# The decode stage of a hybrid attention step: order of loads, masks on another engine, softmax in pieces

## Chip, core and metric

The kernel runs on one core of a Trainium2 chip. The metric is the device time of one execution in microseconds (us). Names of engines: PE is TensorE (PEld its weight loads), DVE is VectorE, ACT is ScalarE, POOL is GpSimd, SP is SyncE, which issues plain DMAs. All data of the stage in question is 32-bit floating point.

## What is computed

One step of a decoder layer: attention in three branches (compressed, selected, local window), a state-space branch, and an MLP, for a prompt of 1024 tokens and for 8 sample sequences of 4 new tokens each behind 4096 cached ones. The change lies in the samples' attention, cut here to what matters:

```
kc = compress(k_all, ...); vc = compress(v_all, ...)                  # 255 compressed rows a sequence
o_cmp, p_cmp = attend_shared(q, kc, vc, dist, dist >= 0, table)
idx, ok = select_blocks(jnp.sum(p_cmp, axis=2), q_pos, ...)           # 16 of the 64-row blocks
o_slc = slc_sample(q, k_slc, v_slc, idx, ok, q_pos, cache_k_slc, cache_v_slc, layer, page_table, table)
o_win, nbk, nbv = win_sample(q, k_win, v_win, cache_k_win[layer], cache_v_win[layer], q_pos, past_len, table)

def masked_softmax(s, mask):
    s = jnp.where(mask, s, NEG_INF)
    p = jnp.where(mask, jnp.exp(s - jnp.max(s, axis=-1, keepdims=True)), 0.0)
    return p / jnp.maximum(jnp.sum(p, axis=-1, keepdims=True), TINY)
```

The kernel computes the selected branch densely: scores against all 4096 cached keys, a mask that is added for the blocks not chosen, one softmax over 4128 columns (32 of them for the new rows), and products with all cached values.

## The kernel before

The stages run one after the other, each ending at a barrier of all engines: inputs, state-space, projections, compression, prompt attention, decode (`stage_decode`), tail (mixing, MLP, output). Only decode and a small preparation of gather indices in `table_steps` are touched.

Decode treats the 8 sequences as two halves of 4 (`NBAT`, `M`; in the text half 0 and half 1, `b` in the code). The rows of a half's score tiles `Ss[b]` (selected, 128 x 4128), `Sw[b]` (window, 128 x 544) and `Sc[b]` (compressed, 128 x 256) are its 4 sequences times 32 queries.

Keys. SP loads the local window of each sequence (256 KB) into four slots `kwin`, the profile's vslc and kT, in runs of one 512-byte row. POOL gathers the paged keys and values with indirect DMAs of 1 MB, 128 rows of 8 KB (16 tokens each), into a ring of 8 slots (`ring`, the last one in the profile under the name bt). There are 32 such gathers: 0 to 7 are half 0's keys, 8 to 15 half 1's, 16 to 23 half 0's values, 24 to 31 half 1's. Gathers 0 to 7 wait for nothing; 8 to 23 wait until PE has turned the keys in their slot, 24 to 31 until the value products have read it (`values_read`). SP's queue holds the windows in order: half 0's keys, half 1's keys (each when its slot is turned), half 0's values, half 1's values.

Key loop. For each half there are nine groups `y`: group 0 is the window, groups 1 to 8 take a quarter of a ring slot of each of the four sequences. PE transposes 16 blocks of 128 x 128 into four PSUM banks (L1913, `keys`), ACT copies three of the banks to SBUF (L2036, the profile calls the target qT) and DVE one (L2086, `keep_keys`). PE then multiplies queries with the turned keys of the group before (L1923, `scores`), and DVE copies the 128 x 512 scores out (L2092, `evac`). Groups 1 to 4 read gathers 0 to 3 (8 to 11 for half 1), groups 5 to 8 the next four.

Between the copies stand, in each engine's own written order: first scores with compressed and new keys (`first_scores`), the sums that rank the blocks (`block_sums`, DVE, on `Sc`), the window's bias, maximum and weights, the choice of blocks (`select`). When half 0's last scores are kept, DVE adds the bias of the last columns (`tail_bias`, L2128) and the masks (`selected`, L2133, twice 2048 columns). Half 0's maximum over 4128 columns (`top`, L2070), its exponential on ACT (`softmax`, L2022) and its scaling (`weights`, L2067) stand in half 1's key loop, at groups 4, 5 and 7.

Values. PE transposes the 40 blocks of a half's weights (`turn`, L1945), ACT and DVE copy them out by turns (`keep_turned`, L2027 and L2015), and PE multiplies them with compressed, window and gathered values (L1978). Half 1's own mask, maximum, exponential and scaling run while PE does half 0's products:

```
            act.wait_ge(scores_done, 2 * GRP)
            keep_turned(0)
            softmax(1, 2, Ss[1][:, :])
            act.wait_ge(values_done, 1)
            keep_turned(1)
```

## Time and profile before

| | us |
|---|---|
| median of 3 runs | 2231.59 (2225.74 to 2232.64) |
| span of the profiled execution | 2226.2 |
| decode in it, first DMA to the tail's first | 918.27 to 1052.73 |
| PE busy over the span | 2067.7 (93%) |
| DVE, ACT, POOL busy over the span | 906.0, 767.3, 559.4 |

The page gives the profiled execution by its span, from the first to the last instruction; no other time of it is noted. The span lies 5.4 us below the median of the runs.

How to read it: PE's 93% is an average that the long products of the tail and the projections set. Decode is some 134 us, in which no engine is busy throughout, and it is read from the timeline (start, duration, engine, line, operation, and in brackets how long the engine stood before it and whom it waited for) and from tables of stretches.

### The profile page before, as it was taken

To read this page: it belongs to the slowest core of one execution; us is meant where nothing else is said; L and a number is where in the kernel's file an instruction comes from. 1 tells how busy PE (TensorE), PEld (TensorE's weight loads), DVE (VectorE), ACT (ScalarE), POOL (GpSimd) and SP (SyncE) were. 2 spreads that over 40 slices of the span, in tenths; PEclk is the share of its full clock that TensorE was granted. 3 is DMA by queue.
4 is the path that set the end of the run, shared out by engine and by line. 5 is a ranking of instruction groups with operands and counts; after the bars stand their busy time and mean duration, and the time that the engine had idled before them with its cause. 6 is when DMAs were issued, how large, how long until landed. Compare 5 with 4: busy or idle time off the path is not lost.

```text
span 2226.2 us, 33758 instructions
## 1 busy us (share of the span) xinstructions
PE 2067.7 (93%) x13984; PEld 1864.4 (84%) x13984; DVE 906.0 (41%) x1720; ACT 767.3 (34%) x1557; POOL 559.4 (25%) x455
## 2 busy tenths in 40 slices
PE   6978899889979999686999999999999999999997
PEld 4755599878856767455999999999999999999997
DVE  4764131146566677375411124454124214313414
ACT  4130321145546777452422232333013113202313
POOL 0640000055433554322212212112212221222120
PEclk8976889989978999799999999999999999999999
DMA  9203035275313223566411113111111111111111
GB/s 354 90 1 121 10 71 114 48 265 193 148 45 84 77 57 83 206 248 258 134 48 48 43 44 116 43 44 38 49 47 48 48 40 46 48 48 38 48 58 78
DMA packets 217072, 201.97 MB, mean 91 GB/s; under 512 B 37174, under 2 KB 199966, under 8 KB 208264
## 3 DMA queue, kind: packets, MB, share of 16 engines
q1 hardware_dynamic: 205126, 131.82, 20.4%
q0 software_dynamic: 9216, 67.11, 7.9%
q8 instruction: 111, 1.82, 0.3%
q10 hardware_dynamic: 2578, 0.88, 0.2%
q14 instruction: 41, 0.34, 0.1%
HBM read 178.05 MB, written 21.58 MB: 90 GB/s over the span
## 4 chain that ended last, share of the span: by engine, by line
PE 51%; DMA 1%; DVE 0%; ACT 0%; POOL 0%; SPq 0%; issue 0%; ACTq 0%; DVEq 0%
PE ps L2216 17%; PE ps L2214 17%; PE ps L2215 17%; PE ps L2360 1%; DMA tail<-x_keep 1%; PE ps L2381 0%; DMA tail<-in_w_br_ssm 0%; POOL tail L2612 0%; DVE tail L2701 0%; SPq L2326 0%; ACT tail L2545 0%; DVE tail L2643 0%; ACT tail L2459 0%; ACTq L2241 0%; ACT tail L2489 0%
## 5 line engine op out<-in xcount | busy, mean ns | idle before, releaser
L2214 PE MATMUL ps<-tail,tail 128*128 128x356 f32 (+2 forms) x2304 | 756.6, 328 | 9.7 <-POOL tail L2612 9.7
L2216 PE MATMUL ps<-tail,tail 128*128 128x356 f32 (+2 forms) x2304 | 750.5, 326 | 0.0
L2215 PE MATMUL ps<-tail,tail 128*128 128x356 f32 (+2 forms) x2304 | 748.6, 325 | 0.0
L2612 POOL TENSOR_TENSOR tail<-tail,tail 128x1024 fp32r<-128x1024 f32 x96 | 232.3, 2420 | 924.6 <-ACT tail L2459 924.6
L2214 PEld LDWEIGHTS ps<-tail,tail 128*128 128x128 f32 x2304 | 435.4, 189 | 12.4 <-POOL tail L2612 9.9
L2215 PEld LDWEIGHTS ps<-tail,tail 128*128 128x128 f32 x2304 | 435.6, 189 | 2.5
L2216 PEld LDWEIGHTS ps<-tail,tail 128*128 128x128 f32 x2304 | 435.8, 189 | 0.0
L2459 ACT ACTIVATE tail<-tail 128x1024 fp32r<-128x1024 f32 x96 | 101.0, 1053 | 320.6 <-PE ps L2216 314.6
L2643 DVE SCALAR_TENSOR_TENSOR tail<-ps,mod,tail 128x346 f32<-128x346 f32 (+2 forms) x120 | 68.7, 573 | 346.7 <-PE ps L2216 336.6
L1669 POOL TENSOR_SCALAR pr<-pr,row_reciprocals,gT 128x640 f32<-128x640 f32 (+7 forms) x128 | 98.7, 781 | 144.7 <-DVE row_reciprocals L1795 142.1
L2514 ACT ACTIVATE tail<-tail,tail 128x346 f32<-128x346 f32 (+2 forms) x96 | 55.9, 583 | 195.5 <-DVE tail L2683 100.1
L1364 DVE TENSOR_TENSOR x_lo<-ps,x_hi 128x512 fp32r<-128x512 f32 (+1 forms) x136 | 85.9, 671 | 80.6 <-ACT x_hi L1328 79.7
L2626 DVE TENSOR_TENSOR tail<-tail,tail 128x346 f32<-128x346 f32 (+2 forms) x48 | 28.9, 601 | 208.9 <-ACT tail L2479 208.9
L2677 DVE TENSOR_TENSOR tail<-ps,tail 128x346 f32<-128x346 f32 (+2 forms) x96 | 50.4, 525 | 154.1 <-PE ps L2216 95.1
L1328 ACT ACTIVATE x_hi<-ps 128x512 fp32r<-128x512 f32 (+1 forms) x136 | 72.7, 582 | 89.2 <-PE ps L1283 89.0
L1730 ACT ACTIVATE pr<-ps,nmax 128x640 f32<-128x640 f32 (+7 forms) x128 | 90.1, 704 | 22.0 <-DVE nmax L1774 20.6
L2214 PE MATMUL ps<-h_lo,w_hi 128*128 128x352 f32 x264 | 88.9, 337 | 9.3 <-DVE w_lo L1154 9.3
L1774 DVE TENSOR_REDUCE nmax<-ps 128x1 f32<-128x640 f32 (+7 forms) x128 | 90.6, 708 | 4.5
L1593 PE MATMUL ps<-consts,pr 128*128 128x128 f32 (+6 forms) x592 | 90.1, 278 | 0.2
L2216 PE MATMUL ps<-h_hi,w_hi 128*128 128x352 f32 x264 | 87.9, 333 | 0.0
L2215 PE MATMUL ps<-h_hi,w_lo 128*128 128x352 f32 x264 | 87.9, 333 | 0.0
L1283 PE MATMUL ps<-consts,byg 128*128 128x128 f32 (+1 forms) x544 | 72.3, 278 | 12.8 <-DMA byg<-out 7.2
(489 smaller groups left out, 2988.7 us busy)
## 6 DMA issues: line engine op xcount, KB each, us to landing
tail<-in_w_ff SPq DMA_DIRECT2D x64, 512.0 KB, 3.9
wada_late<-in_w_ada SPq DMA_DIRECT2D x32, 512.0 KB, 4.0
wada<-in_w_ada SPq DMA_DIRECT2D x4, 2048.0 KB, 11.9
tail<-in_w_in SPq DMA_DIRECT2D x16, 512.0 KB, 3.6
x_keep<-xT SPq DMA_DIRECT2D x1, 4224.0 KB, 23.8
h_keep<-hT SPq DMA_DIRECT2D x1, 4224.0 KB, 11.5
tail<-x_keep SPq DMA_DIRECT2D x1, 4224.0 KB, 13.7
xrow<-in_x_prompt SPq DMA_DIRECT2D x8, 512.0 KB, 8.4
```

The source lines that it names most:

```text
L1283: mm = pe.transpose(bank[y % 4][:, o:o + m], byg[0:m, i % 2, half, g, s:s + 2, :].rearrange("p s d -> p (s d)"), e.ident[0:m, 0:m])
L1328: act.activation(to, src, ACT.Copy).then_inc(hi_kept, 1)
L1364: dve.tensor_tensor(to, src, move(i, b, xhi)[1], ALU.subtract).then_inc(lo_kept, 1)
L1593: mm = pe.transpose(b[0:n, (t % 4) * P:(t % 4 + 1) * P], pr[:, u % NPR, t * n:(t + 1) * n], e.ident)
L1669: pool.tensor_scalar(p, p, rinv[:, k:k + 1], gT[:, qb, h:h + 1], ALU.mult, ALU.mult).then_inc(scaled, 1)
L1730: act.activation(p, score(s), ACT.Exp, bias=nmax[:, s % 4:s % 4 + 1], accum_out=rsum[:, sum_at(s):sum_at(s) + 1]).then_inc(exps_done, 1)
L1774: dve.tensor_reduce(nmax[:, u % 4:u % 4 + 1], s, AXX, ALU.max, negate=True).then_inc(maxima_done, 1)
L2214: pe.matmul(out, whi[:, kw, :], xlo(kx), start=(i == 0), stop=False)
L2215: pe.matmul(out, wlo[:, kw, :], xhi(kx), start=False, stop=False)
L2216: mm = pe.matmul(out, whi[:, kw, :], xhi(kx), start=False, stop=(i == n - 1))
L2459: act.activation(whi[:, x % 2], wraw[:, x % 2], ACT.Copy).then_inc(w_hi, 1)
L2612: pool.tensor_tensor(wlo[:, x % 2], wraw[:, x % 2], whi[:, x % 2], ALU.subtract).then_inc(w_split, 1)
```

## The change

Six things, all in decode but the first:

- `table_steps` makes a second table of row indices, `rowfine`, for half-size rows of 4 KB (8 tokens): index 2r for the first half of row r, 2r+1 for the second, for the columns of gathers 0 to 3.
- The windows of keys and values are laid out with four successive tokens in a partition, so that SP's loads move runs of 2 KB. The window's bias and mask are added with the columns in that order.
- POOL waits for the four first windows before it issues a gather. Gathers 0 to 3 are each split in two, the four first halves ahead of the four second ones. PE waits for the first halves at group 1 and for the second ones at group 3.
- The masks and the tail's bias move from DVE to POOL, into its queue of gathers: behind gathers 11, 15, 19 and 23.
- Maximum and exponential of the 4128 columns are cut in four (`partial_max`, `join_max`, `part`). Half 0's pieces stand between the key copies of half 1's groups 3 to 5 (maxima) and 6 to 8 (exponentials); the scaling follows the loop (`join_sums`, two pieces). Half 1's maxima and exponentials stand ahead of `keep_turned(0)`.
- PE turns a half's weights before it waits for the outputs of the half before.

The diff, cut to its core:

```
+        early = pf[:, 0:2 * FINE].rearrange("p (m h) -> p m h", h=2)[:, :, 0]
+        for s in range(2):
+            dve.tensor_scalar(pfine[:, s, :], early, 2.0, float(s), ALU.mult, ALU.add).then_inc(row_index_step, 1)
+        dve.wait_ge(row_index_step, 5)
+        dve.tensor_copy(e.rowfine[:, :], pfine[:, :, :].rearrange("p s m -> p (s m)")).then_inc(row_index_step, 1)
...
-                sp.dma_start(slots[n % M], cache[0, n].rearrange("(j p) g d -> p j (g d)", p=P)).then_inc(landed[n % M], 16)
+                sp.dma_start(slots[n % M], cache[0, n].rearrange("(p j) g d -> p j (g d)", j=4)).then_inc(landed[n % M], 16)
...
+            def mask(b, half):
+                v = Ss[b][:, half * PAST // 2:(half + 1) * PAST // 2].rearrange("p (s j c) -> p s j c", s=CHK, c=4)
+                k = scs[b][:, half * 32:half * 32 + 32].unsqueeze(1).unsqueeze(3).to_broadcast([P, CHK, 32, 4])
+                pool.wait_ge(selection_step[b], 2)
+                if half == 0:
+                    pool.wait_ge(scores_kept, GRP * b + 5)
+                else:
+                    pool.wait_ge(scores_kept, GRP * (b + 1))
+                    last = Ss[b][:, PAST // 2:PAST].rearrange("p (s c) -> p s c", c=P)[:, :, P - 8:P]
+                    pool.tensor_tensor(last, last, e.btail[:, :].rearrange("p (c s) -> p s c", s=CHK), ALU.add).then_inc(tails_added, 1)
+                    pool.wait_ge(tails_added, b + 1)
+                pool.tensor_tensor(v, v, k, ALU.add).then_inc(masked, 1)
+
+            for m in range(M):
+                load_wait(pool, window_keys_landed[m], 1)
+            for s in range(2):
+                for m in range(M):
+                    pool.indirect_dma_start(ring[m][:, s * CHK // 2:(s + 1) * CHK // 2, :].rearrange("p s x -> p (s x)"), None, fine_rows,
+                                            bass.IndirectOffsetOnAxis(ap=e.rowfine[:, s * M + m:s * M + m + 1], axis=0))\
+                        .then_inc((first_halves, ring_landed)[s][m], 16)
+            for x in range(M, NBAT * 16):
...
+                if 8 <= x < 24 and m == M - 1:
+                    mask((x - 8) // 8, half)
...
-                    elif (y - 1) % 4 == 0:
+                    elif b == 0 and y == 1:
+                        load_wait(pe, first_halves[m], 1)
+                    elif (y - 1) % 4 == 0 or (b == 0 and y == 3):
...
             for b in range(NBAT):
+                for y in range(NG):
+                    turn(b, y)
                 if b:
                     pe.wait_ge(outputs_kept, b)
                 pe.wait_ge(selection_step[1], 2)
-                for y in range(NG):
-                    turn(b, y)
...
+            def part(b, i):
+                act.wait_ge(maxima_done[b], 3)
+                s = Ss[b][:, i * QW:(i + 1) * QW]
+                act.activation(s, s, ACT.Exp, bias=st[:, b, 2:3], accum_out=parts_sum[:, b, i:i + 1]).then_inc(exps_done[b], 1)
...
-                    if b and y == 5:
-                        softmax(0, 2, Ss[0][:, :])
+                    if b and y >= 6:
+                        part(0, y - 6)
+            part(0, 3)
             act.wait_ge(scores_done, 2 * GRP)
+            for i in range(4):
+                part(1, i)
             keep_turned(0)
-            softmax(1, 2, Ss[1][:, :])
...
+            def partial_max(b, i):
+                dve.wait_ge(masked, 2 * b + (1 if i < 2 else 2))
+                dve.tensor_reduce(mx[:, b, i:i + 1], Ss[b][:, (0, 1024, 2048, 3072, W)[i]:(0, 1024, 2048, 3072, W)[i + 1]], AXX, ALU.max).then_inc(partial_maxima, 1)
...
+                if b:
+                    partial_max(0, 0)
                 for y in range(4, GRP):
-                    if b and y == 4:
-                        top(0, 2, Ss[0][:, :])
-                    if b and y == 7:
-                        weights(0, 2, Ss[0][:, :])
                     keep_keys(b, y)
                     evac(b, y - 1)
+                    if b and y == 4:
+                        partial_max(0, 1)
+                    if b and y == 5:
+                        partial_max(0, 2)
+                        partial_max(0, 3)
+                        join_max(0)
                 evac(b, GRP - 1)
-                if b == 0:
-                    tail_bias(0)
-                    selected(0, 0)
-                    selected(0, 1)
+            join_sums(0)
+            for i in range(4):
+                partial_max(1, i)
+            join_max(1)
             dve.wait_ge(scores_done, 2 * GRP)
             keep_turned(0)
-            tail_bias(1)
-            selected(1, 0)
-            selected(1, 1)
-            top(1, 2, Ss[1][:, :])
-            weights(1, 2, Ss[1][:, :])
+            join_sums(1)
             outputs(0)
```

How the instructions stand on the engines that the rest of the text speaks of. POOL in decode, before: the 32 gathers, keys (in_cache_k_slc) and then values (in_cache_v_slc), nothing else.

```order
L1892 DMA ring<-in_cache_k_slc,rowidx 128x2048 x7
L1892 DMA bt<-in_cache_k_slc,rowidx 128x2048
L1892 DMA ring<-in_cache_k_slc,rowidx 128x2048 x7
L1892 DMA bt<-in_cache_k_slc,rowidx 128x2048
L1892 DMA ring<-in_cache_v_slc,rowidx 128x2048 x7
L1892 DMA bt<-in_cache_v_slc,rowidx 128x2048
```

POOL in decode now, up to the first mask of half 1: eight half gathers through rowfine, then whole ones with the masks (Ss with scs) and the tail's bias (Ss with btail) between them.

```order
L1917 DMA ring<-in_cache_k_slc,rowfine 128x1024 x8
L1927 DMA ring<-in_cache_k_slc,rowidx 128x2048 x3
L1927 DMA bt<-in_cache_k_slc,rowidx 128x2048
L1927 DMA ring<-in_cache_k_slc,rowidx 128x2048 x4
L1911 TENSOR_TENSOR Ss<-Ss,scs 128x2048
L1927 DMA ring<-in_cache_k_slc,rowidx 128x2048 x3
L1927 DMA bt<-in_cache_k_slc,rowidx 128x2048
L1909 TENSOR_TENSOR Ss<-Ss,btail 128x16x8
L1911 TENSOR_TENSOR Ss<-Ss,scs 128x2048
L1927 DMA ring<-in_cache_v_slc,rowidx 128x2048 x4
L1911 TENSOR_TENSOR Ss<-Ss,scs 128x2048
```

Each mask stands behind four gathers and ahead of the next four. ACT from the middle of half 1 on, before: L2036 copies keys, L2022 is a softmax's exponential, L2027 copies turned weights.

```order
L2036 ACTIVATE qT<-ps 128x512 x9
L2022 ACTIVATE Ss,st<-Ss,st 128x4128
L2036 ACTIVATE qT<-ps 128x512 x9
L2027 ACTIVATE qT<-ps 128x512 x4
L2027 ACTIVATE wt_end<-ps 128x512
L2022 ACTIVATE Ss,st<-Ss,st 128x4128
L2027 ACTIVATE qT<-ps 128x512 x4
L2027 ACTIVATE wt_end<-ps 128x512
```

ACT now, from the first piece of half 0's exponential on: L2080 copies keys, L2066 is a piece, L2071 copies turned weights.

```order
L2066 ACTIVATE Ss,parts_sum<-Ss,st 128x1032
L2080 ACTIVATE qT<-ps 128x512 x3
L2066 ACTIVATE Ss,parts_sum<-Ss,st 128x1032
L2080 ACTIVATE qT<-ps 128x512 x3
L2066 ACTIVATE Ss,parts_sum<-Ss,st 128x1032 x6
L2071 ACTIVATE qT<-ps 128x512 x4
L2071 ACTIVATE wt_end<-ps 128x512
L2071 ACTIVATE qT<-ps 128x512 x4
L2071 ACTIVATE wt_end<-ps 128x512
```

Six pieces stand in a row: the last two of half 0 and all four of half 1, ahead of the first copies of turned weights. DVE at the end of half 1's key loop, before: the last score copies (L2092), half 0's turned weights (L2015), then half 1's tail bias, masks and maximum.

```order
L2092 COPY Ss<-ps 128x512 x2
L2015 COPY qT<-ps 128x256
L2015 COPY qT<-ps 32x128
L2015 COPY qT<-ps 128x128
L2015 COPY qT<-ps 128x512 x3
L2015 COPY wt_end<-ps 128x384
L2015 COPY wt_end<-ps 32x128
L2128 TENSOR_TENSOR Ss<-Ss,btail 128x16x8
L2133 TENSOR_TENSOR Ss<-Ss,scs 128x2048 x2
L2070 TENSOR_REDUCE st<-Ss 128x1
```

DVE there now: L2138 is the score copy, L2183 to L2189 sum and scale half 0, L2175 and L2179 are half 1's maxima and their join, L2054 copies half 0's turned weights.

```order
L2138 COPY Ss<-ps 128x512 x2
L2183 TENSOR_REDUCE st<-parts_sum 128x1
L2185 TENSOR_SCALAR st<-st 128x1
L2186 RECIPROCAL st<-st 128x1
L2189 TENSOR_SCALAR Ss<-Ss,st,gate_columns 128x2048
L2189 TENSOR_SCALAR Ss<-Ss,st,gate_columns 128x2080
L2175 TENSOR_REDUCE mx<-Ss 128x1 x4
L2179 TENSOR_REDUCE st<-mx 128x1
L2054 COPY qT<-ps 128x256
L2054 COPY qT<-ps 32x128
L2054 COPY qT<-ps 128x128
L2054 COPY qT<-ps 128x512 x3
```

Half 0's scaling has moved from inside the loop to its end, and half 1's maxima from behind half 0's turned weights to ahead of them.

## Rows read from the trace of the kernel before

**Rows 1.** Stretches: length, busy us by engine (instructions), PE clock, DMA share, GB/s.

```profile
917.50:941.00 23.50, 4.78 (x28) 3.26 (x29) 2.05 (x7) 1.19 (x2) 7.59 (x8) 0.60 0.92 359
...
930.00:932.00 2.00, 1.11 (x4) 0.71 (x4) 0.00 (x0) 0.35 (x1) 0.00 (x0) 0.50 1.04 429
```

**Rows 2.** Timeline, key windows: start, length, engine, line, operation [stood before, for].

```profile
918.27 1.71 SPq L1870 DMA_DIRECT2D vslc<-in_cache_k_win  x3
...
921.74 0.66 PE L1913 MATMUL ps<-consts,vslc 128*128 128x128 f32 x4 [2.21 <-DMA vslc<-in_cache_k_win]
...
940.30 1.11 PE L1913 MATMUL ps<-consts,kT 128*128 128x128 f32 x4 [8.69 <-DMA kT<-in_cache_k_win]
```

**Rows 3.** Timeline of POOL's gather issues, and L1892's summary of issue to landing.

```profile
918.96 1.04 POOL L1892 DMA_INDIRECT ring<-in_cache_k_slc,rowidx  x1 [6.27 <-POOLq L66]
...
968.73 1.15 POOL L1892 DMA_INDIRECT bt<-in_cache_k_slc,rowidx  x1 [0.30 <-issue]
...
DMA to landing us min/median/max: 5.4/10.4/18.2
```

**Rows 4.** Timeline, half 0's weights, group 5, its end, half 1's start.

```profile
953.77 0.56 DVE L2067 TENSOR_SCALAR Sw<-Sw,st,gate_columns 128x544 f32<-128x544 f32 x1
...
956.75 0.60 PE L1913 MATMUL ps<-consts,bt 128*128 128x128 f32 x4
...
967.96 0.69 DVE L2092 COPY Ss<-ps 128x512 f32<-128x512 f32 x1 [0.17 <-PE ps L1923]
...
969.09 4.62 DVE L2133 TENSOR_TENSOR Ss<-Ss,scs 128x2048 f32<-128x2048 f32 x2
...
976.01 2.79 PE L1913 MATMUL ps<-consts,ring 128*128 128x128 f32 x12 [4.91 <-DVE qT L2086]
...
976.32 0.35 DVE L2096 TENSOR_SCALAR kT<-kT,st 128x256 f32<-128x256 f32 x1
```

**Rows 5.** Timeline, half 0's softmax inside half 1's loop, and its last copy.

```profile
988.29 4.44 DVE L2070 TENSOR_REDUCE st<-Ss 128x1 f32<-128x4128 f32 x1
...
996.35 3.73 ACT L2022 ACTIVATE Ss<-Ss,st 128x4128 f32<-128x4128 f32 x1
...
999.98 0.19 ACT L2022 ACTIVATION_READ_ACCUMULATOR Ss<-Ss,st 128x1 f32 x1
...
1001.55 2.43 DVE L2067 TENSOR_SCALAR Ss<-Ss,st,gate_columns 128x4128 f32<-128x4128 f32 x1
...
1008.09 0.69 DVE L2092 COPY Ss<-ps 128x512 f32<-128x512 f32 x1 [0.17 <-PE ps L1923]
```

**Rows 6.** Timeline, turned weights, first products, gather 24, wait for gather 31.

```profile
1008.71 0.60 ACT L2027 ACTIVATE qT<-ps 128x512 f32<-128x512 f32 x1 [1.85 <-PE ps L1945]
...
1013.72 0.65 PE L1978 MATMUL ps<-vc,qT 128*32 128x128 f32 x16 [0.93 <-DVE wt_end L2015]
...
1020.92 0.94 POOL L1892 DMA_INDIRECT ring<-in_cache_v_slc,rowidx  x1 [11.73 <-PE ps L1978]
...
1046.49 0.30 PE L1978 MATMUL ps<-bt,qT 128*32 128x128 f32 x1 [0.94 <-DMA bt<-in_cache_v_slc,rowidx]
```

**Rows 7.** POOL's two-operand instructions: L2612's summary (ns), one with a spread operand.

```profile
L2612 POOL TENSOR_TENSOR tail<-tail,tail x96: 2353/2393/4012, 1058.6 to 2186.8; 128x1024 fp32r<-128x1024 f32 x96
...
118.92 1.06 POOL L430 TENSOR_TENSOR ossmT<-ossmT,w 128x512 f32<-128x512 f32 x1
```

**Rows 8.** Timeline: POOL and DVE side by side; two summaries (min/median/max ns).

```profile
1027.13 2.69 POOL L1892 DMA_INDIRECT ring<-in_cache_v_slc,rowidx  x1 [0.31 <-issue]
...
1079.08 3.37 POOL L2612 TENSOR_TENSOR tail<-tail,tail 128x1024 fp32r<-128x1024 f32 x1 [8.01 <-ACT tail L2459]
...
1080.89 1.94 DVE L2626 TENSOR_TENSOR tail<-tail,tail 128x346 f32<-128x346 f32 x1 [0.68 <-ACT tail L2479]
...
L2626 DVE TENSOR_TENSOR tail<-tail,tail x48: 520/528/2726, 1080.9 to 1344.8; 128x346 f32<-128x346 f32 x16, 128x356 f32<-128x356 f32 x16, 128x354 f32<-128x354 f32 x16
...
L2677 DVE TENSOR_TENSOR tail<-ps,tail x96: 518/526/530, 1463.3 to 2113.1; 128x346 f32<-128x346 f32 x32, 128x356 f32<-128x356 f32 x32, 128x354 f32<-128x354 f32 x32
```

More of the change, by code:

```diff
@@ L870, in _ @@
                 tt(e.ossmT[:, f, :], e.ossmT[:, f, :], zT[:, f, :], ALU.mult).then_inc(S["gated"], 1)
+FINE = 4
 def table_steps(nc, e, sb, sem):
@@ L1818, in stage_decode @@
     TCMP, TWIN, TSLC = 0, 2, 7
+    QW = W // 4
     NTL = TSLC + 33
@@ L1856, in stage_decode @@
             "selection_step", "maxima_done", "exps_done", "weights_scaled"))
-        rows_kept, rows_turned = sem("rows_kept"), sem("rows_turned")
+        rows_kept, rows_turned, tails_added, masked = sem("rows_kept"), sem("rows_turned"), sem("tails_added"), sem("masked")
+        first_halves = [sem(f"first_half_landed{i}") for i in range(M)]
+        partial_maxima = sem("partial_maxima")
+        mx = sb("mx", [P, NBAT, 4])
+        parts_sum = sb("parts_sum", [P, NBAT, 4])
         orow = sb("orow", [P, P])
@@ L1884, in _ @@
         def _(pool):
-            for x in range(NBAT * 16):
+            def mask(b, half):
[18 more added lines that the diff above has]
+            for x in range(M, NBAT * 16):
                 kv, b, half, m = x // 16, x // 8 % 2, x // 4 % 2, x % 4
@@ L2123, in select, with join_max, join_sums @@
                 dve.sem_inc(selection_step[b], 1)
[L2125 to L2133 removed]
+            def partial_max(b, i):
+                dve.wait_ge(masked, 2 * b + (1 if i < 2 else 2))
+                dve.tensor_reduce(mx[:, b, i:i + 1], Ss[b][:, (0, 1024, 2048, 3072, W)[i]:(0, 1024, 2048, 3072, W)[i + 1]], AXX, ALU.max).then_inc(partial_maxima, 1)
+            def join_max(b):
+                dve.wait_ge(partial_maxima, 4 * b + 4)
+                dve.tensor_reduce(st[:, b, 2:3], mx[:, b, :], AXX, ALU.max, negate=True).then_inc(maxima_done[b], 1)
+            def join_sums(b):
+                dve.wait_ge(exps_done[b], 6)
+                link(dve.tensor_reduce(st[:, b, 5:6], parts_sum[:, b, :], AXX, ALU.add))
+                x = st[:, b, 5:6]
+                link(dve.tensor_scalar(x, x, 1e-30, None, ALU.max))
+                link(dve.reciprocal(x, x))
+                for i in range(2):
+                    s = Ss[b][:, (0, 2048, W)[i]:(0, 2048, W)[i + 1]]
+                    dve.tensor_scalar(s, s, x, gd[:, b, 1:2], ALU.mult, ALU.mult).then_inc(weights_scaled[b], 1)
             def keep_turned(b):
```

19 lines of the change are left out of this document (8 added, 11 removed).

## Prediction

> **What bounds the kernel now.** I read the profile from the outside in. The table by stage comes first [rows 1]: decode begins at about 917.5 us, the MLP tail starts behind it at a barrier, so every microsecond by which decode ends later or earlier is one of the whole time, and only decode is changed. Its first 23.5 us are transfer: DMA share 0.92, PE busy 4.78. Behind them PE and the two copying engines work in turn, and the end is transfer again, as the last rows show.
>
> The first limit is seen in the window rows [rows 2]. The four local key windows are asked for from 918.27 on. PE had the first at 921.74, but waited 8.69 us for the fourth, until 940.30: its 512-byte pieces pass one by one between 8 KB pieces of the gathers, the first of which POOL issued at 918.96 [rows 3]. Everything gathered had then nearly landed, and half 0 ran at the pace of its engines: its last score copy starts at 967.96 [rows 4]. I call this E0.
>
> Half 1 has three stalls that half 0 lacks. VectorE masks half 0's scores for 4.62 us before it takes up half 1, and PE, which stood 4.91 us for that, comes back slower: 12 transposes in 2.79 us against 4 in 0.60 [rows 4]. Then the 4.44 us maximum, the 3.73 us exponential and the 2.43 us scaling of 4128 columns stand between key copies [rows 5]. From half 0's window scaling at 953.77 to E0 half 0 needs 14.2 us; half 1 has its maximum begin at the same place (988.29) 0.6 us further on and its last copy starts at 1008.09 (E1): 19.8 against 13.6, so 6.2 us of stalls.
>
> The last limit is a ring. The second half of the value gathers of half 1 can only start when the first value products have freed ring slots: POOL waited 11.73 us and issued at 1020.92 (X); the products waited for the last of it until 1046.49, 25.6 us later [rows 6]. So the end of decode hangs on X, and X on how soon half 0's value products run: E1 to X is 12.8 us now.
>
> **The change part by part.** *Windows first, gathers behind, the first four halved.* Windows alone should land as the first did, 3.5 us after the issue (918.27 to 921.74): the fourth issue is at about 920.0, so POOL starts near 923.5, 4.5 us later than now. Twelve issues of about 1.3 us (1.04 in the first row, 0.30 between two) are quicker than the transfer. Transfer starts about 2.4 us after the issue (5.4 us to landing at best [rows 3], less the 2.5 us that a megabyte takes at 429 GB/s [rows 1] and a little). From 925.9 on 8.39 MB of gathers have to pass, and beside them 2.1 MB of further windows: half 1's keys and half 0's values, which SP may now issue as soon as PE has turned the first windows, before 928. With 2 KB against 4 KB pieces, piece by piece, they take a third and are through when the halves are. 10.5 MB at 0.42 MB/us is 25 us, and about one goes to the landing: the last is near 952 (947 if the windows came last, 954 and later if the rate is nearer to the stage's mean of 359). PE has then turned what came before, so group 5 of half 0, whose fourth block is turned at 956.75 now [rows 4], is turned at about 952.1. **Gain 4.6 us on E0** (2 to 8).
>
> *Masks off VectorE.* First scores of half 1 follow the last copy directly: 4.6 us less, and PE does not stand still, which saves 12 x (0.23 - 0.15) = 1.0 and a little on the score products behind them, 1.3 together. But POOL pays. Its two-operand instruction takes 2.39 us for 1024 columns and 1.06 for 512 with a spread operand [rows 7], so 2048 columns cost 4.2 to 4.8 us; I take 4.5 with a small tail addition ahead. In the queue it stands behind four gather issues; in half 0 the last of these ended at 969.88, 1.9 us after E0 [rows 3, 4]. So the mask runs from E0+2.3 to E0+6.8. The block sums of half 1 come up at E0+2.7 or so (now 976.32, 2.6 after the first scores could start at 973.7).
>
> Do they run beside it? The tail shows what happens: a POOL instruction at 1079.08 took 3.37 us instead of 2.39, since VectorE was in a two-operand instruction, and VectorE's next one, at 1080.89, took 1.94 instead of 0.53: it ended when POOL had ended plus its own time [rows 8]. The 96 additions of L2677, with one operand in PSUM, never exceed 0.53 us. It is the same the other way round with a wide scaling of VectorE: POOL's gather issue at 1027.13 took 2.69 us instead of 0.94, beside the second scaling of the kind of 1001.55 [rows 5, 8]. So block sums (both operands in SBUF) and scalings take turns with a mask; key copies from PSUM go on. The block sums lose E0+6.8 less E0+2.7, some of it slack: **+3.3** (0 to 4.5), since the next key copy stands behind them on VectorE and PE behind that copy. The Trainium skill, "GPSIMD Engine Reference", section 8 (Key points), says that POOL shares its SBUF interfaces with VectorE and collides with instructions of two SBUF inputs or in a two-port mode. That speaks against masks on POOL; by it the maxima, with one operand in SBUF and no such mode, go free as well, where no row here has one beside POOL. If they too had to wait, the sum below would be the same, as two of them stand behind the mask anyway.
>
> *Maximum and exponential in pieces.* The 6.2 us go; in their place come four maxima of 1.25 us (4.44/4 and a start) between VectorE's copies and four exponentials of 1.2 us (3.73/4, the 0.19 of the accumulator read [rows 5], a start) between ScalarE's. A group has 2.9 us (11.2 from 956.75 to E0 for three and an end), VectorE's two copies take 1.4 of it; one piece fits, though the copy behind it waits, two pieces and the join do not. I take 1.9 of new stalls (0 to 4). **E0 to E1 gains 4.6+1.3+6.2-3.3-1.9 = 6.9**, E1 is 11.5 earlier, near 996.6.
>
> *What now stands between E1 and X.* Before: ScalarE copied half 0's turned weights at once (from 1008.71), the products started at 1013.72, half 1's softmax ran beside them. Now ScalarE has half 1's four exponentials ahead of those copies, and they need half 1's maximum, hence the POOL mask. The work that hid the softmax is behind it now. The chain, from E1: 2.0 to the mask (last issues, tail addition); mask 4.5 and half 0's scaling 2.4, which fall due together and go one after the other; then two maxima (2.5) or, if the mask came first, four (5.0), and the join 0.3: 11.7 to 14.2, I take 13.0. Four exponentials 4.9. Turned weights 5.0 as now (1008.71 to 1013.72), up to 7 because PE has stood for some 10 us and its 24 left transposes then go at 0.23: I take 6.0, some being turned already. Products to the freed slots: 7.2 now, 6.0 taken, since the value rows have long landed (5.5 to 7.2). Sum 29.9, against 12.8: **loss 17.1** (13 to 20).
>
> *Behind X* the 25.6 us stay, with an idle DMA queue ahead of them: 0.7 less (0 to 1.5). Half 1's weights are scaled and turned by then, which PE's new order allows; that shortens nothing, as the gathers come last. Four small index instructions on VectorE near 332 us, and the new order of window columns, move nothing that is waited for: 0 (to +1).
>
> Sum: -4.6-6.9+17.1-0.7 = +4.9 us. The profiled execution's span is 2226.2, the runs' median 2231.6; the difference is taken over to the median: **2236.5**.
>
> **The rivals.** *A, faster: POOL and VectorE do not collide here.* For: VectorE may come first at both places and POOL's mask fit behind. Against: block sums are of the same kind as the stalled row. Then 3.3 goes, the chain behind E1 falls to 2.0+4.5+2.5+0.3 = 9.3, 3.7 less: 2229.5. Faster by 0.3% (6.7 us) only if the first keys gain 8 (3.4 more) and the turned weights take 4.5 (1.5 more) besides: 2224.6.
>
> *B, slower: the masks cost POOL more than its plain rows.* Their spread operand has runs of four columns, for which I have no row of this length. Each microsecond above 4.5 counts twice, at the block sums and at the mask of half 1. From 5.4 us on the result is over 0.3% slower; at 7 us it is +9.9: 2241.5. Against: the spread row of 1.06 us per 512 is rather fast.
>
> *C, slower: the early keys do not come.* The wait for the windows and the 2.1 MB beside the halves use up the start. For: the same bytes pass, the bus is full in either order, and 4.5 us of it pass before the first gather. Then E0 stays: 2241.1.
>
> **How the numbers follow.** My forecast, the sum as it stands, has 0.50, A 0.12, B 0.23, C 0.15. About 0.3% is what a measurement can tell from no change, and +4.9 is 0.22%. Half of A (0.06) is faster than that, half within it; B and C are above; of the forecast 0.03 crosses the line upward. Faster 0.06, same 0.47 + 0.06 = 0.53, slower 0.23 + 0.15 + 0.03 = 0.41. The range from 2228 to 2245 takes in A without its extras, B and C; about a tenth is left out at either end.
>
> **What would show it.** Gathered keys turned from about 934 instead of 941; E0 near 963.4, not 968; VectorE's first scaling of the block sums in half 1 at 3 us or more instead of 0.35; the POOL masks at 4.2 to 4.8; E1 near 997; ScalarE's exponentials of half 1 ending near 1014 and only then the turned copies; X near 1026 and the products' last wait ending near 1051.5 instead of 1046.5. Wrong would be: masks beside unharmed block sums (A), masks above 5.4 us (B), E0 at 967 or later (C), or X before 1020.

## The result and the profile after

The changed kernel takes 2237.53 us (median of 20 runs), the kernel before 2229.47 beside it: ratio 1.0042, 95% interval 1.0025 to 1.0059, so it is slower by 5.6 to 13.2 us. Decode itself, from the first window's issue to the tail's first load, takes 140.19 us in the profiled execution (919.02 to 1059.21) instead of 134.46: 5.7 more, where 4.9 were forecast. The spans of the two profiled executions differ by 7.5 us, the medians by 8.1; in the profiled one decode began 0.75 us later and the tail took 1.0 more, with unchanged code, and why is not shown. Since decode begins anywhere from 906 to 926 us in the executions below, I count from its first issue.

The front. Timeline rows of the changed kernel (start, length, engine, line, operation [stood before, for]); they answer [rows 2, 3].

```profile
919.02 1.30 SPq L1885 DMA_DIRECT2D vslc<-in_cache_k_win  x3
...
921.74 0.79 PE L1952 MATMUL ps<-consts,vslc 128*128 128x128 f32 x4 [1.47 <-DMA vslc<-in_cache_k_win]
922.82 2.36 PE L1952 MATMUL ps<-consts,vslc 128*128 128x128 f32 x8 [0.29 <-DMA vslc<-in_cache_k_win]
...
925.49 1.05 POOL L1917 DMA_INDIRECT ring<-in_cache_k_slc,rowfine  x1 [11.85 <-DMA vslc<-in_cache_k_win]
...
932.14 1.11 PE L1952 MATMUL ps<-consts,ring 128*128 128x128 f32 x4 [6.11 <-DMA ring<-in_cache_k_slc,rowfine]
...
954.06 0.66 PE L1952 MATMUL ps<-consts,bt 128*128 128x128 f32 x4 [1.82 <-DMA bt<-in_cache_k_slc,rowidx]
...
965.32 0.69 DVE L2138 COPY Ss<-ps 128x512 f32<-128x512 f32 x1 [0.17 <-PE ps L1962]
```

The windows are there within 6 us and gathered keys are turned from 932, but PE then waits for the last gather until 954.06, and E0 (965.32) is 46.3 us after the first issue, where it was 49.7: 3.4 gained.

Half 1's loop, answering [rows 4, 5].

```profile
967.67 3.84 POOL L1911 TENSOR_TENSOR Ss<-Ss,scs 128x2048 f32<-128x2048 f32 x1
...
969.61 2.06 DVE L2142 TENSOR_SCALAR kT<-kT,st 128x256 f32<-128x256 f32 x1
971.71 0.27 DVE L2146 TENSOR_TENSOR sc<-kT 128x64 f32<-128x64 f32 x1
...
974.05 1.53 PE L1952 MATMUL ps<-consts,ring 128*128 128x128 f32 x12 [2.42 <-DVE qT L2132]
...
986.53 2.37 DVE L2175 TENSOR_REDUCE mx<-Ss 128x1 f32<-128x1024 f32 x2
...
986.76 3.85 POOL L1911 TENSOR_TENSOR Ss<-Ss,scs 128x2048 f32<-128x2048 f32 x1 [1.43 <-DVE Ss L2138]
...
989.76 1.09 PE L1952 MATMUL ps<-consts,ring 128*128 128x128 f32 x8 [0.42 <-DVE qT L2132]
...
996.11 0.69 DVE L2138 COPY Ss<-ps 128x512 f32<-128x512 f32 x1 [0.17 <-PE ps L1962]
```

The scaling of 256 columns took 2.06 us instead of 0.35 and ended at 971.67, just behind POOL's mask (971.51). Two maxima at 986.53 took their usual 1.2 us each beside another mask. PE's waits for copies in this half add up to 3.0 us (2.42, 0.16, 0.42) instead of 8.9. E1 is 30.8 us behind E0, not 40.1.

E1 to X and the end, answering [rows 5, 6].

```profile
997.75 6.48 DVE L2189 TENSOR_SCALAR Ss<-Ss,st,gate_columns 128x2048 f32<-128x2048 f32 x2
998.44 4.69 POOL L1911 TENSOR_TENSOR Ss<-Ss,scs 128x2048 f32<-128x2048 f32 x1
1004.15 4.62 DVE L2175 TENSOR_REDUCE mx<-Ss 128x1 f32<-128x1024 f32 x4
1009.06 1.16 ACT L2066 ACTIVATE Ss<-Ss,st 128x1032 f32<-128x1032 f32 x1 [11.92 <-DVE st L2179]
...
1013.62 1.06 ACT L2071 ACTIVATE qT<-ps 128x512 f32<-128x512 f32 x2
...
1019.67 0.64 PE L2017 MATMUL ps<-vc,qT 128*32 128x128 f32 x16 [0.93 <-DVE wt_end L2054]
...
1025.43 0.95 POOL L1927 DMA_INDIRECT ring<-in_cache_v_slc,rowidx  x1 [22.30 <-PE ps L2017]
...
1050.77 0.42 PE L2017 MATMUL ps<-bt,qT 128*32 128x128 f32 x1 [1.87 <-DMA bt<-in_cache_v_slc,rowidx]
...
1059.21 1.31 SPq L2382 DMA_DIRECT2D tail<-in_w_br_attn  x2
```

This is the forecast chain link by link: scaling and mask one after the other, maxima, exponentials, only then the turned copies. E1 to X is 29.3 us instead of 12.8. From X the last gather needs 25.3, against 25.6 before; but from there to the tail it takes 8.4 us, not 6.2.

### The profile page after: what moved, and what is told of

Its sections match the earlier page's. It is cut to its first block, busy times and chain, and to the rows that moved or that the text cites. A ratio compares the mean times of both kernels' runs of the same rounds, so it can differ in the third digit from the quotient of the medians.

```text
span 2233.7 us, 33797 instructions
## 1 busy us (share of the span) xinstructions
PE 2072.2 (93%) x13984; PEld 1867.1 (84%) x13984; DVE 903.1 (40%) x1729; ACT 769.3 (34%) x1569; POOL 578.7 (26%) x465
## 4 chain that ended last, share of the span: by engine, by line
PE 50%; DMA 1%; DVE 0%; ACT 0%; SPq 0%; issue 0%; ACTq 0%; DVEq 0%
PE ps L2272 16%; PE ps L2270 16%; PE ps L2271 16%; PE ps L2416 1%; DMA tail<-x_keep 1%; DMA tail<-in_w_in 1%; PE ps L2437 0%; DVE tail L2781 0%; ACT tail L2610 0%; DVE tail L2757 0%; SPq L2382 0%; SPq L2395 0%; ACT tail L2601 0%; DVE tail L2699 0%; ACT tail L2515 0%
## 5 line engine op out<-in xcount | busy, mean ns | idle before, releaser
L2270 PEld LDWEIGHTS ps<-tail,tail 128*128 128x128 f32 x2304 | 435.5, 189 | 12.9 <-POOL tail L2668 9.7
L1292 PE MATMUL ps<-consts,byg 128*128 128x128 f32 (+1 forms) x544 | 73.3, 281 | 12.9 <-DMA byg<-out 7.3
```

What stands on the lines that cost most here:

```text
L1292: mm = pe.transpose(bank[y % 4][:, o:o + m], byg[0:m, i % 2, half, g, s:s + 2, :].rearrange("p s d -> p (s d)"), e.ident[0:m, 0:m])
L2270: pe.matmul(out, whi[:, kw, :], xlo(kx), start=(i == 0), stop=False)
```

## Experiments

E0 and E1 are the starts of the last score copies of half 0 and half 1, X is the issue of gather 24. All times in this table are from one profiled execution of each kernel, in us: E0 from the first window's issue, E0 to X, X to the tail's first load, and their sum; behind them the ratio to the kernel before of all runs, with its interval.

| kernel | E0 | E0 to X | X to tail | sum | ratio |
|---|---|---|---|---|---|
| before | 49.7 | 53.0 | 31.8 | 134.5 | |
| changed | 46.3 | 60.1 | 33.8 | 140.2 | 1.0042 (1.0025 to 1.0059) |
| e1 turned copies first | 46.7 | 52.8 | 34.1 | 133.6 | 0.9978 (0.9956 to 1.0001) |
| e2 masks on VectorE | 49.2 | 66.5 | 34.6 | 150.2 | 1.0049 (1.0023 to 1.0076) |
| e3 loads only | 47.7 | 52.0 | 31.6 | 131.3 | 0.9986 (0.9963 to 1.0008) |
| e4 whole softmax | 46.3 | 49.0 | 34.0 | 129.3 | 0.9991 (0.9966 to 1.0016) |
| e5 busy waits | 45.3 | 61.6 | 31.9 | 138.8 | 1.0013 (0.9991 to 1.0034) |
| e6 early softmax | 45.9 | 43.7 | 32.9 | 122.5 | 0.9947 (0.9923 to 0.9972) |
| e7 runs only | 42.5 | 53.1 | 31.3 | 126.9 | 0.9959 (0.9938 to 0.9979) |
| e8 together | 44.0 | 43.9 | 32.7 | 120.7 | 0.9955 (0.9932 to 0.9978) |
| e9 halves, no wait | 46.8 | 52.5 | 32.0 | 131.3 | 1.0007 (0.9984 to 1.0030) |
| e10 wait, no halves | 48.2 | 53.0 | 31.3 | 132.5 | 1.0010 (0.9984 to 1.0036) |
| e11 late windows | 41.5 | 43.8 | 31.8 | 117.1 | 0.9915 (0.9887 to 0.9942) |
| e12 late and halves | 42.3 | 44.1 | 31.7 | 118.1 | 0.9929 (0.9902 to 0.9955) |

### Is the ring's loss the order? (e1, e4)

```diff
+            keep_turned(0)
             for i in range(4):
                 part(1, i)
-            keep_turned(0)
```

> The changed kernel with one thing altered: ScalarE and VectorE copy half 0's turned weights ahead of half 1's maxima and exponentials. My account (the 29.3 us from E1, half 0-like last score copy of half 1 at 996.11, to X, the issue of gather 24 at 1025.43, are half 1's softmax standing ahead of half 0's turned weights): the copies can begin when half 0's weights are scaled (1004.2), X follows some 11 us later near 1015, 10 us earlier than in the changed kernel, and the end moves with it: about 2227.5 us, 10 below the changed kernel. Rival 1 (the waiting is not the order but the collision of mask and scaling): X stays past 1020 and the time above 2233. Rival 2 (X moves, but half 1's weights are then last): X near 1015, but VectorE still scales half 1's weights after gather 31 has landed, and the time stays near 2237.

Measured 2228.13 us, 9.4 below the changed kernel's median. VectorE's copies were moved in the same way. Timeline rows of this run:

```profile
1003.91 6.49 DVE L2189 TENSOR_SCALAR Ss<-Ss,st,gate_columns 128x2048 f32<-128x2048 f32 x2
1004.60 4.70 POOL L1911 TENSOR_TENSOR Ss<-Ss,scs 128x2048 f32<-128x2048 f32 x1
...
1015.47 1.08 PE L2017 MATMUL ps<-vc,qT 128*32 128x128 f32 x16 [0.93 <-DVE wt_end L2054]
...
1022.96 0.95 POOL L1927 DMA_INDIRECT ring<-in_cache_v_slc,rowidx  x1 [13.65 <-PE ps L2017]
```

The collision of scaling and mask is still there (6.49, 4.70), yet X follows the last score copy by 20.7 us instead of 29.3: the order was 8.6 of the 16.5 us lost, and rivals 1 and 2 fall. The other 7.9 stay: half 0's scaling, which stood inside the loop before, now starts 1.6 us behind the last score copy and needs 6.5 with the mask in between, and only then can the turned weights begin.

For the other side, e4 puts the maximum, the exponential and the scaling of half 0 back whole (4128 columns at groups 4, 5 and 7), and half 1's behind the turned copies:

```diff
-                    if b and y >= 6:
-                        part(0, y - 6)
-            part(0, 3)
+                    if b and y == 5:
+                        softmax(0, 2, Ss[0][:, :])
             act.wait_ge(scores_done, 2 * GRP)
-            for i in range(4):
-                part(1, i)
             keep_turned(0)
+            softmax(1, 2, Ss[1][:, :])
...
```

> The changed kernel with half 0's maximum, exponential and scaling whole again at their old places in half 1's loop, and half 1's softmax behind half 0's turned weights as before; loads and POOL masks stay. My account (the pieces shorten E0 to E1 but bring the softmax of half 1 between E1 and X): E0 to E1 is about 36, some 5 longer than the changed kernel's 30.8, E1 to X falls back from 29.3 to about 13, so X comes some 11 us earlier, and the time is 2223 to 2228, below the changed kernel and the kernel before. Rival (the pieces are a gain and the loss is POOL's masks): slower than the changed kernel by the 5 us, about 2242.

E0 to E1 was 36.3 and E1 to X 12.7, both as my account had it; the time, 2228.8, lies 0.8 above its range, less than the runs scatter, and can't be told from the kernel before. So the pieces gain 5.5 us in the loop (36.3 less 30.8), and what came with them, half 1's softmax ahead of the turned copies and half 0's scaling behind the loop, loses 16.6 (29.3 less 12.7).

### What do the masks cost? (e2)

```diff
+                if b == 0:
+                    tail_bias(0)
+                    selected(0, 0)
+                    selected(0, 1)
...
+            tail_bias(1)
+            selected(1, 0)
+            selected(1, 1)
             for i in range(4):
                 partial_max(1, i)
...
```

> The changed kernel with the masks and the tail's bias back on VectorE, half 0's at the end of its key loop as in the kernel before, half 1's ahead of its maxima. My account (POOL's mask costs the block sums only the 1.7 us by which their first scaling was lengthened, and spares 4.6 of mask and about 1.3 of PE's slow return): E0 to E1 grows from 30.8 to about 35, E1 to X from 29.3 to about 30, time about 2242.5. Rival (a mask beside VectorE costs VectorE as much as one of its own): E0 to E1 stays at about 31 and the time at 2237.5.

Measured 2243.68 us, 6.2 above the changed kernel's median, near my account; but the two intervals overlap, so the runs alone can't tell them apart. In the stretches E0 to E1 is 35.1 and E1 to X 31.4. VectorE in that run:

```profile
976.72 4.62 DVE L2166 TENSOR_TENSOR Ss<-Ss,scs 128x2048 f32<-128x2048 f32 x2
...
983.95 0.35 DVE L2127 TENSOR_SCALAR kT<-kT,st 128x256 f32<-128x256 f32 x1
```

Without a mask on POOL the scaling is back at 0.35 us: the 1.7 us were the collision. POOL's masks are a gain in the loop, as forecast, and a larger one: 4.3 us from E0 to E1, where the prediction's terms give 2.6 (4.6 and 1.3 less 3.3), and 2.1 more from E1 to X. The sum in the table differs by 10.0, but 2.9 of that lies ahead of E0, and no run shows it to be a price of the masks: the last gather landed 35.1 us after the first issue, as in the changed kernel (35.0), and the 100 matrix instructions behind it took 14.08 us at a clock of 0.79, against 11.26 at 1.00 there (that row stands further down, under the landings).

```profile
961.42:975.50 14.08, 14.08 (x100) 8.55 (x100) 4.84 (x8) 5.75 (x10) 2.35 (x3) 0.79 0.65 249
```

### Why is the end 2 us slower? (e5)

The same 130 products stand behind the last gather in each kernel. Tables of stretches (length, busy us of PE, PEld, DVE, ACT, POOL with their counts, granted clock, DMA share, GB/s): the changed kernel from its last wait on, then the kernel before from its own.

```profile
1050.00:1055.00 5.00, 4.23 (x80) 3.92 (x84) 0.00 (x0) 0.00 (x0) 0.00 (x0) 0.50 0.00 0
...
1050.77:1057.00 6.23, 6.20 (x130) 5.38 (x130) 0.00 (x0) 0.00 (x0) 0.00 (x0) 0.64 0.01 3
```

```profile
1046.49:1050.60 4.11, 4.03 (x130) 3.56 (x130) 0.01 (x1) 0.00 (x0) 0.00 (x0) 1.00 0.00 0
```

```profile
1040.83 5.39 PE L2017 MATMUL ps<-ring,qT 128*32 128x128 f32 x126 [2.08 <-DMA ring<-in_cache_v_slc,rowidx]
...
1048.32 0.58 PE L2017 MATMUL ps<-ring,qT 128*32 128x128 f32 x2 [2.09 <-DMA ring<-in_cache_v_slc,rowidx]
```

In the kernel before, half 1's weights were turned later: its first products began at 1038.41, 17.5 us behind X, against 10.2 in the changed kernel, and PE stood only 0.94 us for the last gather [rows 6]. The experiment fills those waits with idle work:

```diff
+                                if b:
+                                    for i in range(8):
+                                        pe.transpose(bank[4][:, 0:P], e.ident, e.ident)
                                 load_wait(pe, ring_landed[x % NR], x // NR + 1)
```

> The changed kernel with eight idle transposes (into a bank nobody reads) ahead of each of the waits for half 1's value gathers, so that TensorE doesn't stand still there. Theory (the 2.2 us by which the changed kernel needs longer from the last wait's end to the tail, 8.44 against 6.24, are the clock: it was granted 0.50 in the last products, because TensorE had stood about 2 us before each gather): the clock is near 1.0 in the last products, last wait to tail 6.3 us, the whole 2 us shorter, 2235.5. Rival (the products are slower for another reason, such as the transfer or the order of the turned weights): last wait to tail stays at 8.4 or grows, the time stays at 2237.5 or rises by the transposes.

```profile
1053.99 0.30 PE L2017 MATMUL ps<-bt,qT 128*32 128x128 f32 x1 [0.20 <-DMA bt<-in_cache_v_slc,rowidx]
```

```profile
1054.00:1058.00 4.00, 4.00 (x130) 3.56 (x130) 0.00 (x0) 0.00 (x0) 0.00 (x0) 1.00 0.02 4
```

The first row is the last wait in the timeline of this run, the second the stretch behind it. The clock is 1.00 and the last wait to the tail takes 6.28 us, as before the change. The whole took 2234.61; the 2 us cannot be told from the runs alone, but the stretch shows them.

### Which part of the new loads gains? (e3, e7, e9, e10)

The three parts of the new loads on the kernel before (the runs as in e7 below, the wait as here, the halves as in the change):

```diff
+            for m in range(M):
+                load_wait(pool, window_keys_landed[m], 1)
+            for s in range(2):
+                for m in range(M):
+                    pool.indirect_dma_start(ring[m][:, s * CHK // 2:(s + 1) * CHK // 2, :]...
...
-            for x in range(NBAT * 16):
+            for x in range(M, NBAT * 16):
...
```

> The kernel before with the loads alone changed: windows in 2 KB runs, POOL waiting for the first four of them, the first four gathers halved; masks, softmax and orders as before. My account: E0 comes 3.4 us earlier, counted from the first window's issue (46.3 instead of 49.7, as in the changed kernel), nothing behind it changes, and the time is 3.4 us below the kernel before, about 2226. Rival (the gain is lost at the next limit, since half 1's gathers or the ring set X): E0 earlier, X not, time as before, 2229.5.

E0 was 47.7, the rest as before, and 2228.71 us with an interval that holds both theories: inconclusive in time. E0 gains less than in the changed kernel, though the last gather landed as early (34.8 us after the first issue, 35.0 there); the 100 matrix instructions behind it took 12.8 us instead of 11.3. So I took the parts singly. The runs of 2 KB alone, on the kernel before:

```diff
-                sp.dma_start(slots[n % M], cache[0, n].rearrange("(j p) g d -> p j (g d)", p=P)).then_inc(landed[n % M], 16)
+                sp.dma_start(slots[n % M], cache[0, n].rearrange("(p j) g d -> p j (g d)", j=4)).then_inc(landed[n % M], 16)
...
```

> The kernel before with the windows in 2 KB runs and nothing else: POOL issues its gathers at once, none is halved. Theory (the fourth window came late because its small pieces took turns with those of the gathers, and larger pieces get a larger share): PE has the fourth window 22 us after the first issue no more, but within about 8 to 10; E0 is 2 to 3.4 us earlier than before's 49.7, as with the wait and the halves, and the time is up to 3 us below the kernel before, about 2227. Rival (only waiting with the gathers brings the windows forward): the fourth window still after 15 us or more, E0 within 1 us of 49.7, the time 2229.5.

Measured 2222.96 us: the layout in one line (and the window's bias in that column order) gains 0.41%, 0.21 to 0.62, more than I gave them and more than all the new loads together. PE has the fourth window 11.3 us after the first issue (932.18), not 22, and waits for no gather behind the fourth:

```profile
932.18 1.12 PE L1913 MATMUL ps<-consts,kT 128*128 128x128 f32 x4 [1.94 <-DMA kT<-in_cache_k_win]
...
938.80 1.11 PE L1913 MATMUL ps<-consts,ring 128*128 128x128 f32 x4 [2.48 <-DMA ring<-in_cache_k_slc,rowidx]
```

Then each of the other two with the runs. Without POOL's wait, e9 leaves out the first two lines of e3's diff; without the halves, e10 leaves out the others.

> The kernel with the loads alone changed, without POOL's wait for the windows; runs of 2 KB and halved first gathers stay. Theory W (POOL's wait costs the gain of the runs, since the bus has only the windows to carry while it lasts): E0 about 42.5 us after the first issue, as with the runs alone, the time 7 to 8 us below the kernel before, 2223. Theory H (the halves cost it, since the second halves of the first gathers push gathers 4 to 7 back and PE waits for the last of them): E0 at 46 or later, time near 2228.

> The kernel with the loads alone changed, without the halves; runs of 2 KB and POOL's wait for the windows stay. Theory W (the wait costs the gain): gather 7 lands some 35 us after the first issue as with wait and halves, E0 at 46 to 48, time near 2228. Theory H (the halves cost it): E0 about 43, the time near 2223.

Neither theory holds alone: e9 came out as H said and e10 as W said. Each addition by itself takes the gain away (2231.31 and 2231.11 us). The landings, read from the increments of the gathers' semaphores, and E0, in us from the first issue (one execution of each kernel):

```
                 window 4   gather 3   gather 7     E0
before             22.0       17.0       27.7      49.7
runs only          11.3       17.9       31.0      42.5
changed             5.6    19.1 (25.0)   35.0      46.3
wait, no halves     5.7       23.4       33.8      48.2
halves, no wait     8.2    13.3 (22.1)   33.1      46.8
late windows       11.4       16.7       27.7      41.5
late and halves     8.9    12.3 (18.2)   28.2      42.3
(with halves: first half, in brackets the second)
```

Two limits explain all but the first row. Without halves E0 is gather 3 and 24.5 to 24.8 us (the rest of group 1, seven groups, the last copy): 17.9, 23.4 and 16.7 give 42.5, 48.2 and 41.5. With halves it is gather 7 and 11.3 us, if PE keeps its clock: the wait shifts gather 3 by 5.5 us, and the halves bring PE ahead of the transfer, so that it stands before gathers 5 to 7 in e9 and pays with its clock. But the halves alone do not settle whether it pays. In the seven kernels with all the new loads (the changed one, e1 to e6) gather 7 landed after 34.0 to 35.4 us; in five of them, where PE had stood 0.34 us at most for gather 6, E0 followed 11.3 later; in e2 and e3, where it had stood 1.44 and 0.69 us, 14.1 and 12.9. So 1.6 to 2.8 us of E0 came from the clock with the same loads. The same 100 matrix instructions from the last gather to E0, in the changed kernel and in e9:

```profile
954.06:965.32 11.26, 11.26 (x100) 6.71 (x100) 4.84 (x8) 5.65 (x10) 6.20 (x4) 1.00 0.84 325
```

```profile
958.52:972.19 13.67, 13.67 (x100) 8.13 (x100) 4.84 (x8) 5.64 (x10) 2.35 (x3) 0.81 0.64 249
```

Why the size of the pieces matters can be counted from the landings. Before, the fourth window landed 9.8 us behind the third (12.2 and 22.0), with 512 pieces; the gathers, 128 pieces each, landed 2.65 us apart meanwhile, which makes some 470 pieces. With 2 KB it was 3.1 us (8.2 and 11.3) for 128 pieces, and a gather landed every 3.1 us. So window and gather pieces passed about one for one, an estimate from these landings: a window of fewer pieces is through sooner.

### Put together (e6, e8, e11, e12)

In e6 half 0's maxima begin in its own loop, its exponentials stand at groups 4 to 7 and its scaling at group 8, ahead of half 1's second mask; the mask of half 0's second half is cut in two and ends before the block sums; the turned copies come first.

```diff
+                    if b and 4 <= y < 8:
+                        part(0, y - 4)
...
+                for lo, hi in {11: ((0, 16), (16, 24)), 13: ((24, 32),)}.get(x, ()):
+                    mask(0, lo, hi)
```

> Put together from the findings: loads as changed; half 0's maxima at the end of its own loop and at half 1's groups 0, 1 and 3, its exponentials at groups 4 to 7, its scaling at group 8 and just behind; the mask of half 0's second half in two pieces, the first ahead of gather 12, the second ahead of gather 14; half 0's turned weights ahead of half 1's softmax. My account (E1 comes early by the pieces, X follows E1 by about 13 us as in the kernel before once the scaling is done at E1, and the end hangs on X): E0 to E1 about 29.5 us, E1 to X about 13, first window's issue to X near 89 where the changed kernel has 106.4 and the kernel before 102.7; with 33.9 from X to the tail the stage takes about 123 us, and the time is near 2218, 0.5% below the kernel before. Rival 1 (maxima between key copies cost as much as they save): E0 to E1 33 or more, time 2222 or more. Rival 2 (half 1's softmax becomes last behind X): X as said, but the products wait for half 1's weights and not for gathers, and the time is above 2223.

Measured 2219.67 us and 122.5 us for the stage, against 2218 and 123: my account. E0 to X is 43.7 us, 16.4 less than in the changed kernel.

```diff
-            for m in range(M):
-                load_wait(pool, window_keys_landed[m], 1)
...
```

The halves leave in the same way, and eight idle transposes come in as in e5.

> The kernel of the early softmax without POOL's wait for the windows and without halved gathers (the 2 KB runs stay), and with eight idle transposes ahead of each wait for half 1's value gathers. My account: E0 as with the runs alone (42.5 us after the first window's issue, where the early softmax had 45.9), E0 to X as there (43.7), X to the tail as with the busy waits (31.6 instead of 32.9): 118 us from the first issue to the tail, where the kernel before has 134.5, so 16 us below it, about 2214, 0.7%. Rival (the gains overlap: what comes earlier at the front meets half 1's gathers that are not there yet): E0 to X grows by the 3 us, time 2217 to 2220.

Measured 2220.0 us: a miss. The rival had the time but not its reason, as E0 to X stayed at 43.9. E0 came at 44.0 and not 42.5, gather 7 only at 32.4. And eight transposes a wait were too many once all came early: PE was through with them 1.3 us after the last gather had landed. The next run therefore has six, and tests what the landings say, that windows wanted some 25 us later pass among the first gathers:

```diff
-                sp.wait_ge(keys_turned, n - M + 1)
+                sp.wait_ge(keys_turned, 6 * M)
...
-                                    for i in range(8):
+                                    for i in range(6):
```

> The kernel of the early softmax with windows in 2 KB runs, no wait of POOL and no halves, six idle transposes ahead of the waits for half 1's value gathers, and SP holding back half 1's key windows and half 0's value windows until PE has turned group 5. Theory (E0 is the landing of gather 7 plus the last groups at 2.9 us each, or of gather 3 plus seven groups; the 2 MB of windows that passed among the gathers delay both): gather 3 lands about 15.5 us after the first issue instead of 18.5, gather 7 at about 26 instead of 32.4, E0 at 40 instead of 44; E0 to X 43.9 as before, X to the tail 31.8: 116 from the first issue to the tail, time about 2214. Rival (half 1's windows are then late): E0 at 40, but PE stands at the start of half 1 for the windows, E0 to X grows by 3 or more, time 2218.

Measured 2213.53 us, 0.9915 (0.9887 to 0.9942), the lowest median of all: 19 us below the kernel before, 24 below the changed one by medians. Gather 7 landed at 27.7 instead of 32.4, E0 came at 41.5 (forecast 40, as gather 3 was there at 16.7 and not 15.5), and half 1 waited 0.43 us for its windows. How much of the gain over e8 is the windows and how much the two transposes fewer, the times don't tell; E0 is 2.5 us earlier, X to the tail 1.0 shorter. The same with halves, as in the change:

```diff
...
-                    elif (y - 1) % 4 == 0:
+                    elif b == 0 and y == 1:
+                        load_wait(pe, first_halves[m], 1)
+                    elif (y - 1) % 4 == 0 or (b == 0 and y == 3):
```

> The same with the first four gathers halved. Theory: the first halves have landed by about 12 us after the first issue, gather 7 by about 27, E0 at 38.5 (27 and four groups), the time 1.5 us below the run without halves, 2212.5. Rival (halves cost PE its clock and the bus its pace, as in the run with halves and no wait, where E0 was 46.8 against 42.5 with the runs alone): E0 at 41 or later, the time at or above the run without halves.

Measured 2214.96 us, which can't be told from e11, and E0 at 42.3: the rival. PE took its first gathered keys early, then stood for gathers 6 and 7 and ran the last 100 instructions at a mean clock of 0.79, so that E0 was 14.1 us behind gather 7 and not 11.3:

```profile
954.37 1.12 PE L1954 MATMUL ps<-consts,bt 128*128 128x128 f32 x4 [1.84 <-DMA bt<-in_cache_k_slc,rowidx]
```

```profile
954.37:968.42 14.05, 14.05 (x100) 8.51 (x100) 5.97 (x8) 5.76 (x10) 6.52 (x4) 0.79 0.91 365
```

## Why the prediction held, and where it did not

The time was 1.0 us from the forecast and the sign of the sum was right, but +4.9 (0.22%) lies just under the measured interval, and the likeliest of my three outcomes, no difference that can be told, is not what came. Part of the closeness is luck: the forecast stood on a median of 2231.6 for the kernel before, which came out as 2229.5 beside the changed one, so by medians the change was +8.1; and in the sum below, misses of +1.2, -2.4, -0.6 and +2.7 nearly cancel. Term by term, forecast and measured in decode:

| step | forecast | measured |
|---|---|---|
| E0 | -4.6 | -3.4 |
| E0 to E1 | -6.9 | -9.3 |
| E1 to X | +17.1 | +16.5 |
| behind X | -0.7 | +2.0 |
| sum | +4.9 | +5.7 |

*E0.* Its mechanism held, its size was a little off: the last gather, not the halves, sets E0, as I had it. From POOL's first issue to the last gather's landing it took 28.5 us, as forecast; but POOL began 6.5 us after the first window's issue and not 5.2, as the fourth window landed only after 5.6 us. What I did not see is that the 2 KB runs alone would do better than all three parts: I named the small pieces, but gave the gain to the three parts together, while the runs of e7, e9 and e10 show that with 2 KB pieces the fourth window is there after 11.3 us beside the gathers, and that the wait and the halves each undo the gain.

*E0 to E1.* The place and the cause of the collision held: mask from E0+2.35, block sums stalled until its end, and e2 without them. The terms were too dear: the mask took 3.84 us, not 4.5, and the block sums came up at E0+4.3, not 2.7, so 1.7 us were lost, not 3.3; the pieces cost PE 0.6 us of waits (0.16 and 0.42) where I took 1.9. Rival A falls by 2.06 against 0.35, rival B by 3.84, rival C by the 3.4 at E0.

*E1 to X.* All links hold within half a microsecond or so: maximum joined at E1+12.8 (13.0), exponentials 4.8 (4.9), turned copies 6.0 (6.0), products 5.8 (6.0). Here masks and half 0's scaling did go one after the other, and the mask itself was stretched to 4.69. By e1 half 1's softmax ahead of the turned copies was 8.6 of the 16.5, half 0's scaling behind the loop, with the mask in its way, the other 7.9; by e6 nearly all can be had back (E1 to X 13.95).

*Behind X.* The step that failed. I had half 1's weights done earlier and wrote that it "shortens nothing"; it lengthened. PE, ready early, stood about 2 us before each of three gathers and then ran the last 130 products at a mean clock of 0.64, 6.20 us instead of 4.03, a loss of 2.2 that the sum had at nothing; with the waits filled they took 4.0 (e5). The 0.7 that the idle queue was to give came out as 0.2.

*The collision in numbers.* The Trainium skill, "GPSIMD Engine Reference", section 8 (Key points), names contention of POOL with VectorE instructions in a two-port mode or with two SBUF inputs. The rows agree for the maxima, which have one input: beside a mask (986.53) they keep their 1.2 us. The scaling of 256 columns, which has one tensor input too, ended only with POOL's whole instruction; whether it ran in a two-port mode no row here shows.

## What to carry to other kernels

When an edit speeds a loop by moving work out of its way, follow that work to the next ring or barrier: here 16.5 us came back, because half 0's moved scaling and half 1's softmax stood ahead of the copies that free the ring. Order transfers by when they are needed: here giving the needed windows larger pieces, and holding back windows wanted some 25 us later, was worth more than making the gathers wait for them. And test the parts of a bundle singly: the 2 KB runs of this one gain 0.4%, two of its other parts undo that.

## What was not expected of the hardware

The fourth 256 KB window in 512-byte pieces beside gathers of 8 KB pieces arrived 22.0 us after the first issue, in 2 KB pieces 11.3, and 5.6 with no gathers beside it. And PE, after standing 0.8 to 2.1 us ahead of each of two or three transfers, ran the next 100 to 130 instructions at a mean clock of 0.64 to 0.81, for 2.2 to 2.8 us more (the changed kernel's end, e2, e9, e12); at the end of the stage idle transposes ahead of each wait kept it at 1.00 (e5). A gather issue on POOL took longer beside VectorE's wide scaling in a changed kernel as in [rows 8]: e8's third one behind X, beside scalings of 2.62 us in all from 1014.49 on.

```profile
1013.40 0.94 POOL L1922 DMA_INDIRECT ring<-in_cache_v_slc,rowidx  x1 [0.30 <-issue]
1014.64 2.58 POOL L1922 DMA_INDIRECT ring<-in_cache_v_slc,rowidx  x1 [0.30 <-issue]
```
